# Half of the last conditioning group summed as slices on VectorE in the last head pair; a third conditioning unit ahead of the first pair

## What is computed

```
def adaln(cond, w, b):
    m = jax.nn.silu(cond) @ w + b
    return jnp.split(m, 6, axis=-1)

x = x + g_m * (ox @ mla_w_out[m])                       # layer 0 mixer
x = x + g_f * ec_moe(modulate(x, norm_ffn[i], sh_f, sc_f), ...)
x = x + g_m * short_conv_mixer(hx, ...)                 # layer 1 mixer
```

## Time and profile before

| quantity | value |
| --- | --- |
| median of 3 runs | 1592.2 us (1591.47 to 1592.33) |
| the profiled execution | 1592.2 us |
| its span, first to last instruction | 1590.4 us |
| mean granted TensorE clock | 0.98 |
| PE busy | 1454.8 us, 91% of the span |
| DVE busy | 668.4 us, 42% |
| ACT busy | 232.3 us, 15% |
| DMA | 504.93 MB, mean 317 GB/s |
| chain that ended last | PE 72%, DMA 20%, DVE 5%, ACT 2% |

### The profile page before, as it was taken

How to read it: one execution, slowest core, us unless ns; L and a number is a source line. 1 busy time by engine, 2 the same in 40 slices (tenths; PEclk the granted TensorE clock), 3 DMA queues, 4 the chain that set the end, 5 groups by cost and what they waited for, 6 DMA issues and landing times.

```text
span 1590.4 us, 15656 instructions
## 1 busy us (share of the span) xinstructions
PE 1454.8 (91%) x6490; PEld 678.2 (43%) x6490; DVE 668.4 (42%) x1161; ACT 232.3 (15%) x430; POOL 80.5 (5%) x72
## 2 busy tenths in 40 slices
PE   4999999999599999999989899999599999998987
PEld 2655656554233333332323588854133333333332
DVE  2576777433713232322322778734423232232223
ACT  3133453333300000000000300013100000000000
POOL 0010010000000000000000033000100000000000
PEclk9999999999889999999999999999699999999999
DMA  9933221496589999999999923452699999999996
GB/s 383 339 120 118 82 104 53 166 391 269 198 344 426 427 426 427 426 428 427 426 427 428 388 71 108 165 218 107 246 428 427 425 427 428 426 427 427 427 427 293
DMA packets 59248, 504.93 MB, mean 317 GB/s; under 512 B 7999, under 2 KB 8222, under 8 KB 29482
## 3 DMA queue, kind: packets, MB, share of 16 engines
q1 hardware_dynamic: 54928, 490.69, 75.1%
q0 software_dynamic: 2752, 8.92, 1.5%
q10 hardware_dynamic: 1498, 4.33, 0.7%
HBM read 497.62 MB, written 6.29 MB: 317 GB/s over the span
## 4 chain that ended last, share of the span: by engine, by line
PE 72%; DMA 20%; DVE 5%; ACT 2%; issue 1%; ACTq 0%; DVEq 0%; POOLq 0%
PE ps L1011 31%; DMA work<-in_exp_w_up_dram 11%; PE ps L1095 9%; PE ps L870 7%; DMA ring<-in_exp_w_up_dram 6%; PE ps L1027 5%; PE ps L617 3%; PE ps L777 3%; PE ps L736 3%; PE ps L679 2%; PE ps L675 2%; PE ps L740 1%; PE ps L763 1%; DMA work<-in_ada_w_dram 1%; PE ps L1049 1%; PE ps L995 1%
## 5 line engine op out<-in xcount | busy, mean ns | idle before, releaser
L1011 PE MATMUL ps<-ring,work 128*64 128x512 f32 x1824 | 409.2, 598 | 31.2 <-ACT work L1355 13.0
L1011 PE MATMUL ps<-work 128*64 128x512 f32 x1248 | 282.5, 601 | 20.9 <-ACT work L1355 8.9
L1890 DVE TENSOR_TENSOR work<-ps,work 128x1024 f32<-128x1024 f32 x120 | 141.3, 1219 | 283.1 <-PE ps L1027 283.1
L1011 PEld LDWEIGHTS ps<-ring,work 128*64 128x64 f32 x1824 | 127.5, 137 | 294.2 <-issue 250.4
L1011 PEld LDWEIGHTS ps<-work 128*64 128x64 f32 x1248 | 87.4, 138 | 202.2 <-issue 172.1
L1027 PE MATMUL ps<-work 64*128 64x512 f32 x480 | 119.3, 615 | 0.0
L1908 DVE SCALAR_TENSOR_TENSOR work<-ps,gate_e,gate_ffn 128x512 f32<-128x512 f32 x32 | 24.0, 751 | 185.8 <-PE ps L1011 185.8
L1901 DVE TENSOR_TENSOR work<-work,ps 128x512 f32<-128x512 f32 x32 | 22.0, 687 | 176.1 <-issue 151.8
L1351 ACT ACTIVATE work<-ps 128x512 f32<-128x512 f32 x32 | 19.1, 597 | 487.3 <-PE ps L1011 487.3
L2078 POOL DMA_INDIRECT work<-xn_rows,row_no x32 | 30.6, 956 | 1036.5 <-PE ps L995 733.2
L1355 ACT ACTIVATE work<-ps 128x512 f32<-128x512 f32 x32 | 19.1, 597 | 372.8 <-PE ps L1049 372.8
(11 more groups left out here) (306 smaller groups left out, 1355.3 us busy)
## 6 DMA issues: line engine op xcount, KB each, us to landing
ring<-in_exp_w_gate_dram SPq DMA_DIRECT2D x38, 2048.0 KB, 31.7
ring<-in_exp_w_up_dram SPq DMA_DIRECT2D x37, 2048.0 KB, 32.4
ring<-in_exp_w_down_dram SPq DMA_DIRECT2D x37, 2048.0 KB, 33.6
work<-in_exp_w_up_dram SPq DMA_DIRECT2D x27, 2048.0 KB, 31.5
work<-in_exp_w_gate_dram SPq DMA_DIRECT2D x24, 2048.0 KB, 34.8
work<-in_exp_w_down_dram SPq DMA_DIRECT2D x23, 2048.0 KB, 36.8
ring<-in_ada_w_dram SPq DMA_DIRECT2D x32, 1024.0 KB, 7.0
ring<-in_ada_w_dram SPq DMA_DIRECT2D x6, 2048.0 KB, 7.6
```

Source lines behind the costliest of these rows:

```text
L1011: last = mm(PS[64 * h:64 * h + 64, bank, :], lhsT[:, m * P + 64 * j:m * P + 64 * j + 64], slot_rows[sl][:, m, h * BANK:(h + 1) * BANK], st ...
L1890: v.tensor_tensor(row, PS[:, b:b + 2, :], row, ALU.add).then_inc(added[L], 1)
```

## The change

- `UNITS` becomes 6, in `UNITS_IN` = [3, 0, 0, 0, 3]. Unit 2 runs ahead of pair 0, from a third buffer in ring 1, and none runs in pair 2. The last pair keeps units 3, 4 and 5: two after scores(0), one after probs_T(0).
- Blocks 4 to 7 of group 4 become four late slices on DVE (`add_late`, 128x2048 each). `add_late(0)` stands first in pair 3, ahead of `top(0, 0)`; `add_late(1)` to `add_late(3)` stand at the ends of t = 0, 1 and 2. DVE still adds unit 3 after `top` of t = 0 and units 4 and 5 at the ends of t = 0 and 1; units 6 and 7 and their adds are gone.
- SP loads these four blocks into `late_w`, the first 32 KB a partition of `work`, where expert chunks 0 and 1 used to be loaded, behind the loads of all units.
- Chunks 0 and 1 are loaded in the mixer, after `slices_sum` has read `late_w[3]`; that sum (four matmuls) stands in PE's first tile of the mixer, with one addition on DVE behind it.

```diff
-    UNITS = (len(GROUPS) - 3) * KC // 2
+    UNITS = 6
-        ada_buf = [view(R[2], h * 2 * GROUP, 2, GROUP) for h in range(2)]
+        ada_buf = [view(t, lo, 2, GROUP) for t, lo in ((R[2], 0), (R[2], 2 * GROUP), (R[1], 0))]
+        late_w = [view(W, n * GROUP, GROUP) for n in range(4)]
-        UNITS_IN = [2, 0, 0, 1, 5]
+        UNITS_IN = [3, 0, 0, 0, 3]
-        GATE_AT = UNITS_IN[0]
-        UNIT_BANK = [2, 0, 7] + [7, 6, 7, 7, 7]
+        UNIT_BANK = [2, 0, 1, 7, 6, 7]
+        UNIT_BUF = [0, 1, 2, 0, 1, 1]
@@ SP
-                if n == GATE_AT:
+                if n == 3:
                     for m in range(KC):
                         if m < 4:
-                            sp.wait_ge(unit_mm, m // 2 + 1)
+                            sp.wait_ge(unit_mm, (1, 1, 2, 3)[m])
...
-                elif n == GATE_AT + 1:
+                elif n == 4:
                     sp.wait_ge(gate_mm, 1)
-                elif n >= 2:
-                    sp.wait_ge(unit_mm, n - 1)
+                elif n == 5:
+                    sp.wait_ge(unit_mm, n)
...
             sp.wait_ge(proj, 10 * PAIRS)
-            load_chunk(0, 0)
-            load_chunk(0, 1)
+            for m in range(4):
+                sp.dma_start(late_w[m], ada_w[1, (4 + m) * P:(5 + m) * P, 2 * D:4 * D]).then_inc(ada_in[m], 16)
             for h, done in ((0, mixw_in[0]), (1, out_half_in)):
-                sp.wait_ge(unit_mm, UNITS - 1 + h)
+                sp.wait_ge(unit_mm, (4, 6)[h])
...
-            for n in (2, 3, 4, 5, 9):
+            for n in (2, 3, 4, 5):
+                load_chunk(0, n)
+            sp.wait_ge(ada_main, FIRST_LOADS + 3)
+            for n in (0, 1, 9):
                 load_chunk(0, n)
@@ PE
                     if i == 2:
-                        pe.wait_ge(unit_added, u + 1)
+                        pe.wait_ge(proj_d, 5 * (i + 2))
                         gate_sum(0, gate_w[1][:, 3, :], 7)
...
-                    unit(u + 3)
                     scores(3)
                     probs_T(2)
-                    unit(u + 4)
                     values(0)
...
-            for n in range(2):
+            for n in range(UNITS_IN[0]):
                 unit(n)
...
                         constant()
+                        if L == 0:
+                            pe.wait_ge(unit_added, UNITS)
+                            slices_sum(2 * KC + 4, late_w[3], 7)
@@ DVE
+            def add_late(m):
+
+                dve.wait_ge(ada_in[m], 16 * (part_loads(4 + m) + 1))
+                if m == 0:
+                    ins = v.tensor_scalar(late_w[0], late_w[0], cond_T[:, 4, 0:1], None, ALU.mult)
+                else:
+                    dve.wait_ge(slice_added, 2 * KC + m)
+                    ins = v.scalar_tensor_tensor(out=late_w[m], in0=late_w[m], scalar=cond_T[:, 4 + m, 0:1], in1=late_w[m - 1],
+                                                 op0=ALU.mult, op1=ALU.add)
+                ins.then_inc(slice_added, 1)
...
                 for t in range(XT):
+                    if i == PAIRS - 1 and t == 0:
+                        add_late(0)
...
-                    if not ahead:
+                    if not ahead and t < 2:
                         add_unit(u + t + 1)
+                    if not ahead and t < 3:
+                        add_late(t + 1)
...
                 add_mix(0, 1)
+                if L == 0:
+                    dve.wait_ge(ada_main, FIRST_LOADS + 3)
+                    v.tensor_tensor(ada_part[0], PS[:, 7, :], ada_part[0], ALU.add).then_inc(ada_rows, 1)
```

More of the change, by code:

```diff
@@ L274, in build @@
         gate_in, gate_added, gate_mm = [sem("gate_in0"), sem("gate_in1")], sem("gate_added"), sem("gate_mm")
-        unit_in = [sem("unit_in0"), sem("unit_in1")]
+        unit_in = [sem("unit_in0"), sem("unit_in1"), ada_in[3]]
         ada_main, ada_rows, ada_sum, ada_out, mod_ready = (sem(n) for n in (
@@ L320, in part_loads, with unit_loads @@
         def part_loads(k):
-            return (4, 4, 3, 1)[k % 4] + k // 4 + 1
+            return (4, 4, 3, 3)[k % 4] + k // 4 + 1
+        def unit_loads(n):
+            return 32 * sum(UNIT_BUF[m] == UNIT_BUF[n] for m in range(n + 1)) + 16 * (UNIT_BUF[n] == 2)
         def unit_of(n):
@@ L420, in _ @@
                 for kk in range(2):
-                    rows, buf = slice((2 * kp + kk) * P, (2 * kp + kk + 1) * P), ada_buf[n % 2][:, kk, :]
+                    rows, buf = slice((2 * kp + kk) * P, (2 * kp + kk + 1) * P), ada_buf[UNIT_BUF[n]][:, kk, :]
                     if L == other:
-                        sp.dma_start(buf, ada_w[L, rows, lo * D:lo * D + GROUP]).then_inc(unit_in[n % 2], 16)
+                        sp.dma_start(buf, ada_w[L, rows, lo * D:lo * D + GROUP]).then_inc(unit_in[UNIT_BUF[n]], 16)
                     else:
                         sp.dma_start(buf.rearrange("p (l n) -> p l n", l=2), ada_w[:, rows, lo * D:(lo + 1) * D].rearrange("l p n -> p l n")
-                                     ).then_inc(unit_in[n % 2], 16)
+                                     ).then_inc(unit_in[UNIT_BUF[n]], 16)
             def load_chunk(L, n):
@@ L530, in ada_product, with slices_sum @@
                 ada_slices(ADA_BANK, first_ada[u], 2 * u, u == 0, u == FIRST_LOADS - 1).then_inc(ada_main, 1)
-            def slices_sum(c, acc_w, bank):
-                pe.wait_ge(slice_added, c * KC)
+            def slices_sum(slices, acc_w, bank):
+                pe.wait_ge(slice_added, slices)
                 for g in range(4):
@@ L645, in unit @@
             def unit(n):
-                pe.wait_ge(unit_in[n % 2], 32 * (n // 2 + 1))
+                pe.wait_ge(unit_in[UNIT_BUF[n]], unit_loads(n))
                 if n == 1:
@@ L656, in unit @@
                     pe.wait_ge(unit_added, n - 1 if n == UNIT_AT[PAIRS] + 1 else n)
-                ada_slices(UNIT_BANK[n], ada_buf[n % 2], 2 * unit_of(n)[1], True, True).then_inc(unit_mm, 1)
+                ada_slices(UNIT_BANK[n], ada_buf[UNIT_BUF[n]], 2 * unit_of(n)[1], True, True).then_inc(unit_mm, 1)
             def project(n, s, units):
@@ L800, in pair @@
                         pe.wait_ge(proj_d, 5 * (i + 2))
-                        slices_sum(2, part_w[3], 7)
+                        slices_sum(2 * KC, part_w[3], 7)
                     if UNITS_IN[i + 1]:
@@ L839, in _ @@
                 if s == 5:
-                    slices_sum(1, ada_acc, ADA_BANK)
+                    slices_sum(KC, ada_acc, ADA_BANK)
             pe.wait_ge(ada_rows, 2)
@@ L977, in mixer_out @@
                     pe.wait_ge(sq, XT)
+                    pe.wait_ge(ada_rows, 4)
                     ada_collect(PAIRS - 1)
```

## The result

| | before | after |
| --- | --- | --- |
| median | 1591.84 us (4 runs) | 1604.86 us (4 runs) |
| lowest to highest | 1589.82 to 1592.33 | 1604.15 to 1608.11 |
| ratio, 95% interval | | 1.0085 [1.0072, 1.0097] |
| span of the profiled execution | 1590.4 | 1606.1 |
| mean granted clock | 0.980 | 0.975 |

The change makes the kernel 13.0 us slower, with an interval of 11.5 to 15.4. In a second comparison of the same two kernels it was 1605.74 against 1592.9 us, a ratio of 1.0082 [1.0068, 1.0095]. The profiled execution of the changed kernel took 1608.11 us and was the slowest of its four, so what is read from its profile adds up to more than the medians differ.

A forecast was written before the change was run, and what follows sets the result against it. The prediction took pair 3 to be bound by a loop of scores, DVE's `top` and ACT's exponential, not PE's work alone. 15.1 + 0.2 - 1.0 + 1.0 = +15.3 us on 1592.2 gave 1607.5 us, range 1603 to 1611.

The forecast's parts named there:

- The load: Pair 3: late slice 0, issued after SP's wait for unit 4, lands at about 321.2; the second `top` starts 15.1 us later.
- The clock: Pair 3, scores(1): after PE's idle gap one restart at half clock loses 2.5 us, bounds 0 and 4.3.
- The third rival: Pair 3: the clock stays low beyond scores(1), through probs_T(0) and into scores(2), up to 1610.8 us; chance 10%.
- +0.2: Pair 3, t = 1: a slice of 2.34 us exceeds DVE's 2.17 us of idle time, 0.2 us slower.
- -1.0: Pair 3, ahead of values(0): removing unit 7 saves 1.0 us, bounds 0 and 1.85.
- Unit 6: Pair 3, between probs_T(1) and scores(3), which ACT released: removing this unit is worth 0.
- +1.0: Mixer, where PE has no gaps: the four matmuls of `slices_sum` add 1.0 us.
- +0.7: Ahead of pair 0: the added unit's PE time is covered, its add on DVE isn't, 0.7 us slower.
- -1.9: Pair 2: the unit removed there lay on the chain of waits, so all that follows comes 1.9 us sooner.
- The first rival: Pair 3: late slice 0 lies in `work` before DVE comes to it, no stall, 1591.2 us; chance 3%.

The follow-up runs named there:

- e1_early: Changed kernel, but SP asks for the four late slices right after the last projection, ahead of its wait for unit 4: 1593.15 us, ratio 1.0000 to before.
- e4_adds_later: Changed kernel with SP as it is, but the four slice adds later in DVE's list, at the ends of t = 1 to 3 and after: 1592.71 us.
- e7_warm15: Changed kernel plus 15 matmuls of 128x512 that nobody reads, on PE behind unit 4, ahead of scores(1): 1603.84 us, ratio 1.0060 to before.
- e2_swap: Changed kernel, but after its wait for unit 4 SP issues the four late slices ahead of unit 5's two loads: 1602.83 us, ratio 1.0060 to before.
- e8_early_buf: e1_early with unit 5 in the buffer of unit 3 instead of unit 4, so asked for sooner: 1589.19 us, and 1589.14 us when run again.
- e5: Kernel before with only unit 2 moved ahead of pair 0 (third buffer), none in pair 2; eight units, no slices: 1589.68 us, ratio 0.9976.
- e6: Kernel before with only expert chunks 0 and 1 loaded in the mixer; eight units, no slices: 1593.52 us, ratio 1.0004.
- e9: e8_early_buf with three slices ahead of pair 3's first maximum, the fourth ending t = 0, `slices_sum` in unit 6's place, not the mixer: 1588.52 us.
- e3: Changed kernel plus 30 matmuls of 128x512 that nobody reads, on PE behind unit 4, ahead of scores(1): 1616.93 us, ratio 1.0148 to before.
- after_again: The changed kernel run again without any edit, beside the kernel before on the same chip: 1605.74 us, ratio 1.0082.

## Why the prediction was right, point by point

The forecast was 1607.5 us in a range of 1603 to 1611; measured were 1604.86 us. The mechanism and its two large terms, the landing and the clock, came as forecast. That the total is so near is in part luck: small terms missed in both directions, and the medians differ by 1.4 us less than the stages add up to.

- **The load.** Expected to land at 321.2, 9.8 us after SP's release; it landed at 321.96, 9.8 us after 312.13. Release and landing are both 0.8 us later than forecast, as pair 3 began at 304.42 and not at 303.65: this execution was 1.6 us later than before at `a` already, and 0.8 us wasn't lost ahead of pair 1. From the start of pair 3 to the second maximum it took 16.4 us more than before, where the prediction's numbers give 16.3. e1_early and e4_adds_later show from two sides that this wait, with the softmax behind it, is the loss: ask earlier or wait later, and it is gone.
- **The clock.** Taken at 2.5 us, measured 3.0 in the trace, of which e7_warm15 gave back 2.87 in the stage. The term was slightly small; in e2_swap, after a shorter pause, the same restart cost 2.1 us. One comparison behind it doesn't hold: 13.6 us is longer than the 5 us from PE's stop to the fall of the clock in the earlier trace rows, but not than the pause of 27 us before the experts (412.9 to 439.85), of which PE was idle for about two thirds. The third rival (the clock stays low through probs_T) didn't happen: it was up at 332, ahead of the transposes at 332.7. They can't have kept it low, and what the Trainium skill says on transposes in "TensorE: Matmul & The Clock Gate", section "Part 4: PE-mode transpose", wasn't put to the test.
- **DVE's slices.** Step "+0.2" in t = 1 was wrong: 332.81 to 340.43 is 7.62 us, the 7.61 of before. The slice ends just as the scores arrive.
- **The units removed.** "-1.0" for unit 7 fits: from the last maximum to the mixer it takes 15.88 us (347.85 to 363.73) against 16.99 (332.00 to 348.99), and 15.88 or 15.89 in every kernel with six units. Unit 6, taken at 0, was worth 0.16: the tile before took 7.42 us instead of 7.58. In e8_early_buf both together, less the 0.25 us that tile 1 is longer there, make the 0.98 by which pair 3 is shorter.
- **The mixer.** "+1.0" was short. Mixer to experts took 1.26 us more: 0.90 us for the sum, and 0.36 us of "issue" ahead of the first modulation (L1902), where before had 0.04 (438.87 to 438.91). In the chain of after:

```profile
367.64 0.90 PE ps L544 x8
...
454.51 0.40 issue
454.91 0.43 DVE work L1902
```

The second piece is in the chain of all nine profiles of kernels with the sum in the mixer, and in none of the four without (before, e5, e6, e9). What it is stays open.
- **Ahead of pair 0.** "+0.7" was right only for some executions. With the clock falling at the same place as in before, a to pair 1 takes 77.60 to 77.62 us (e1, e3, e4) and 78.05 (e5) against 76.82: +0.8 to +1.2. In seven of the eleven profiles that have the third unit it takes 76.75 to 76.78, as before. The chain and the granted clock tell why: in before the scores at 124 ran at the lower clock, in after the later projection did.

```profile
126.09 2.82 PE ps L744 x8
...
164.03 5.38 PE ps L683 x8
```

Before had 4.97 us for those scores and 3.69 for that projection. The clock of before (columns as in Rows 1):

```profile
126.00:128.00 2.00, 2.00 (x4) 1.01 (x3) 0.00 (x0) 0.00 (x0) 0.00 (x0) 0.50 1.01 416
164.00:166.00 2.00, 1.81 (x5) 0.88 (x6) 0.77 (x2) 1.24 (x3) 0.00 (x0) 1.00 0.00 0
```

And of after:

```profile
126.00:128.00 2.00, 1.91 (x6) 1.25 (x7) 0.00 (x0) 0.00 (x0) 0.00 (x0) 1.00 1.03 422
164.00:166.00 2.00, 1.97 (x3) 0.97 (x4) 0.89 (x1) 1.08 (x2) 0.00 (x0) 0.57 0.01 4
```

Every one of the thirteen profiles has the fall at one of the two places (around 122 us, or at 162 to 165) and never at both; at the later one it costs less. That the third unit brings this about, since it fills part of a pause in which PE would stand, is likely but not shown: the fall came late in seven of eleven profiles with it and in neither of the two without.
- **Pair 2.** "-1.9", measured -1.96 in every kernel that has it.
- **The sum.** Stages of after against before add up to -0.07 - 1.96 + 15.17 + 1.26 = +14.4 us; predicted were +15.3, that is +0.7, -1.9, +15.5 (pair 3 reckoned from its own start) and +1.0. The medians say +13.0. The rest, 1.4 us, isn't explained; it lies within the interval (11.5 to 15.4). All kernels with the third unit come out better in the median than in their stages, by 0.2 to 2.8 us: e5_unit_ahead -3.3 where its own stages say -0.5 (ahead of pair 3 alone -0.7; it would be -1.2 there with the +0.8 of e1, e3 and e4, and -2.0 with the later fall of the clock). A likely reason is the clock in stages that the change doesn't touch: between 30 and 42 us it doesn't fall at all in four profiles (e4, e5, e6, e9, `a` at 107.64 to 107.66), once in four (before, e1, e3, e7: 108.50 to 109.44) and twice in five (after, after_again, e2 and both of e8: 109.83 to 110.42). Each kernel has one profiled execution, so how often its other executions have these falls can't be read, and the reason isn't shown.
- **The first rival's price** (1591.2 us without the stall) missed one step. Unit 5's buffer costs 1.5 us, which the stall had covered; only without it does it show (e1_early, 1593.15).

## What to carry to other kernels

Before filling an engine's idle time, ask whether the data is there in that gap: it depends on the list of the engine that issues the load, on each wait ahead of it, and on how many loads stand before it in the queue. An instruction that can be late belongs behind, not ahead of, what others wait for; moving four instructions down a list was worth as much here as moving the loads up (1592.71 and 1593.15 us, each level with before). And when a stall is removed, the next late thing shows (here a buffer chosen one unit too late), so look at the waits again before counting the gain.

## What the runs showed of the hardware beyond what was expected

- The same code ahead of `a` ran with no, one or two falls of the clock from one profile to the next, and `a` moved by 2.8 us with their number (107.64 to 110.42).
- Loads of 1 MB in SP's queue landed in the order of issue, the first after 4.95 us, the third after 9.8 (e2_swap, after): two places in the queue were worth 4.9 us.
- Thirteen microseconds of matmuls that nobody reads made the kernel 1.9 us faster, because they kept the clock at 2.4 GHz over a wait (e7_warm15). The restart at 1.2 GHz that they avoided cost 3.0 us after PE had stood for 13.4 us, and 2.1 us after 8.5 (after, e2_swap).
- In seven of eleven profiles a unit of 1.8 us ahead of pair 0 cost nothing. In these the fall of the clock came not around 122 us, where the scores took 4.97 us instead of 2.82, but at 162 to 165 us, where a projection took 5.38 instead of 3.69.
- A 128x512 fp32 matmul over all 128 columns takes 0.87 us from one to the next (30 in 26.02 us), though one of its rows in the profile is 0.6 us: each is two rows that overlap.
